# The output projection of a hybrid decoder block, computed as seven block products instead of eight

## The reference

```
x  += (sum_i sigmoid(gate_i) * y_i) @ W_o      # the output projection, 1024 x 1024
x  += squared_relu_mlp(rms_norm(x))            # up: 1024 -> 4096, down: 4096 -> 1024
```

## Time and profile before

| | us |
|---|---|
| median of 3 runs | 1169.45 (1169.36 to 1169.71) |
| time of the profiled execution | 1170.08 |
| its span, first to last instruction | 1168.3 |
| TensorE busy | 1152.2 |
| VectorE / ScalarE / GpSimd busy | 660.6 / 528.6 / 392.4 |

### The profile page before, as it was taken

One profiled execution on the slowest core, in us unless ns is written; L12 is line 12 of the kernel. 1 busy time (PEld: TensorE's weight loads), 2 busy tenths in 40 slices (PEclk: granted clock), 3 DMA queues, 4 the chain that ended last, 5 costly groups with the idle time before them and its releaser, 6 DMA issues.

```text
span 1168.3 us, 20827 instructions
## 1 busy us (share of the span) xinstructions
PE 1152.2 (99%) x8686; PEld 944.8 (81%) x8686; DVE 660.6 (57%) x1202; ACT 528.6 (45%) x848; POOL 392.4 (34%) x256
## 2 busy tenths in 40 slices
PE   8999999999999999999999999999999999999998
PEld 7998877978789678767777777778888888888887
DVE  4699526454554552543253475552469469378386
ACT  6455432323323443677454554442654344344452
POOL 3444426243544225323341543244240420511400
PEclk9999999999999999999999999999999999999999
DMA  6213323122321141211621221243161622534421
GB/s 257 91 57 104 113 83 109 65 82 81 107 73 67 56 140 52 92 36 37 238 76 61 75 91 55 72 163 99 64 234 58 267 90 90 221 104 158 166 91 72
DMA packets 39455, 124.06 MB, mean 106 GB/s; under 512 B 4657, under 2 KB 9521, under 8 KB 38850
## 3 DMA queue, kind: packets, MB, share of 16 engines
q1 hardware_dynamic: 33744, 111.17, 27.8%
q10 hardware_dynamic: 5106, 11.43, 2.8%
q0 software_dynamic: 512, 0.13, 0.1%
HBM read 112.01 MB, written 9.04 MB: 104 GB/s over the span
## 4 chain that ended last, share of the span: by engine, by line
PE 82%; DVE 8%; ACT 5%; POOL 2%; issue 2%; DMA 1%; SPq 0%; DVEq 0%; ACTq 0%; POOLq 0%
PE pst L1993 23%; PE pst L1995 22%; PE pst L1994 22%; POOL w_lo L907 1%; PE pst L2507 1%; ACT w_hi L1026 1%; PE pst L2499 1%; PE pst L2232 1%; PE pst L2285 1%; PE pst L2484 1%; PE pst L2469 1%; DVE cdif L1513 1%; PE pst L2219 1%; DVE x_lo L1847 1%; PE pst L2524 1%
## 5 line engine op out<-in xcount | busy, mean ns | idle before, releaser
L907 POOL TENSOR_TENSOR w_lo<-raw,w_hi 128x1024 fp32r<-128x1024 f32 x109 | 270.5, 2487 | 484.4 <-ACT w_hi L1026 472.7
L1993 PE MATMUL pst<-h_hi,w_hi 128*128 128x512 f32 (+1 forms) x704 | 257.1, 365 | 1.3 <-DVE h_lo L1486 0.7
L1995 PE MATMUL pst<-h_hi,w_lo 128*128 128x512 f32 (+1 forms) x704 | 243.2, 345 | 0.0
L1994 PE MATMUL pst<-h_lo,w_hi 128*128 128x512 f32 (+1 forms) x704 | 242.9, 345 | 0.0
L1993 PEld LDWEIGHTS pst<-h_hi,w_hi 128*128 128x128 f32 x704 | 133.4, 189 | 25.9 <-issue 5.4
L1026 ACT ACTIVATE w_hi<-raw 128x1024 fp32r<-128x1024 f32 x127 | 133.0, 1052 | 44.9 <-PE pst L1995 40.8
L1994 PEld LDWEIGHTS pst<-h_lo,w_hi 128*128 128x128 f32 x704 | 133.6, 190 | 15.7 <-issue 2.9
L1995 PEld LDWEIGHTS pst<-h_hi,w_lo 128*128 128x128 f32 x704 | 133.3, 189 | 16.0
L1993 PE MATMUL pst<-x_hi,w_hi 128*128 128x512 f32 (+1 forms) x272 | 102.6, 377 | 0.4 <-DVE x_lo L1859 0.4
L1994 PE MATMUL pst<-x_lo,w_hi 128*128 128x512 f32 (+1 forms) x272 | 102.4, 377 | 0.0
L1995 PE MATMUL pst<-x_hi,w_lo 128*128 128x512 f32 (+1 forms) x272 | 102.4, 376 | 0.0
(11 more groups left out here) (370 smaller groups left out, 2412.9 us busy)
## 6 DMA issues: line engine op xcount, KB each, us to landing
raw<-in_weights SPq DMA_DIRECT2D x127, 512.0 KB, 3.4
raw_late<-in_weights SPq DMA_DIRECT2D x34, 512.0 KB, 4.2
raw_free<-in_weights SPq DMA_DIRECT2D x27, 512.0 KB, 3.6
xt<-in_x SPq DMA_DIRECT2D x4, 512.0 KB, 6.0
wait_gate<-stage ACTq DMA_DIRECT2D x8, 256.0 KB, 2.6
gate_t<-wait_gate ACTq DMA_DIRECT2D x1, 2048.0 KB, 9.2
x<-in_x ACTq DMA_DIRECT2D x1, 2048.0 KB, 8.5
out<-x SPq DMA_DIRECT2D x7, 256.0 KB, 2.1
```

Source lines behind the costliest of these rows:

```text
L907: nc.gpsimd.tensor_tensor(w_lo[:, u % W_SLOTS, :], raw_unit(u), w_hi[:, u % W_SLOTS, :].bitcast(F32), ALU.subtract).then_inc(lo_ready, 1)
L1993: M(out, lh, rh, start=(first and i == 0), stop=onto, skip_group_check=onto)
L1994: M(out, lh, rl, start=False, stop=onto, skip_group_check=onto)
L1995: last = M(out, ll, rh, start=False, stop=(final and i == len(terms) - 1), skip_group_check=onto)
```

## The change

- The output projection is a sequence of 14 jobs `("wo", -1, (m, j))`, seven products m of two units j, in the form of `down`, with an order of its own: 0 (U11), 1 (S1), 2 (S2), 3 (U12), 4 (S4), 5 (S3), 6 (U22). Each job has 12 matmuls of 512 columns. Below, the units are called F to F+13 (product m has F+2m and F+2m+1). Products 1, 2, 5 and 6 take differences of weight units (F+2 to F+5, F+10 to F+13), made on VectorE by `weight_sums`.
- The low parts of these eight units are written by VectorE, those of the six plain ones (F, F+1, F+6 to F+9) by GpSimd.
- `merge_tile` writes the quarters, and for odd k the four sums and their parts, and then does the weight sums and low parts that are due. For `proj` k that is: the difference of F+2 in `merge_tile(2)`, of F+3 in 4, of F+4 and the low part of F+2 in 6; the first `wo` job brings the difference of F+5 and the low part of F+3.
- Products 0 to 4 complete the first two token blocks, 5 and 6 the others. `norm2` of blocks 0 and 1 stands around product 5, that of 2 and 3 behind product 6, among four units of `up_early` (two before), which have banks of their own.
- The ten raw slots are used from unit F on, and the order of the loads is adapted.

The core of the diff (`merge_tile` is that of VectorE; the waits behind it are TensorE's and, last, those of SP's queue):

```diff
+P1, P5, P6, P2, P7, P3, P4 = ((U11, (0, 0)), (S1, (0, 1)), (S2, (1, 1)), (U12, (1, 0)), (S3, (0, 0)), (S4, (1, 1)),
+                              (U22, (1, 0)))
+PRODUCTS = {"wo": [P1, P5, P6, P2, P3, P7, P4], "down": [P1, P5, P6, P2, P7, P3, P4]}
+LESS = {"wo": {1: 0, 2: 1, 5: 2, 6: 2}, "down": {1: 0, 2: 1, 4: 2, 6: 2}}
+BANKS = {"wo": [(4, 5), (6, 7), (4, 5), (1, 3), (6, 7), (4, 5), (4, 5)],
...
+PHASE_O = [("wo", -1, (m, j)) for m in range(NM) for j in range(2)]
+EARLY = 4
...
+FFN0 = UNIT_NO[("w_o", -1, (0, 0))]
...
+DOWN_NO = {u: i for i, u in enumerate(sorted(UNIT_NO[u] for u in UNITS if u[0] == "w_down" or UNIT_NO[u] in LESS_UNIT))}
...
             g("merge_tile", KD - 1)
-            jobs(KD // 2 + 2)
+            jobs(8)
             g("norm2_tables")
-            for b in range(NB):
...
+            jobs(2)
+            g("norm2", 0)
+            jobs(1)
+            g("norm2", 1)
+            jobs(1)
+            g("norm2_turn", 0)
+            g("norm2_turn", 1)
+            g("norm2_low", 0)
+            jobs(1)
+            g("norm2_low", 1)
+            jobs(1)
+            g("up_units")
+            g("up_early", 0)
+            g("norm2", 2)
+            g("up_early", 1)
+            g("norm2", 3)
+            g("norm2_turn", 2)
+            g("norm2_low", 2)
+            g("up_early", 2)
+            g("norm2_turn", 3)
+            g("norm2_low", 3)
+            g("up_early", 3)
...
             def merge_tile(k):
-                dve.wait_ge(m_hi, k + 1)
-                V.scalar_tensor_tensor(out=x_lo[:, k, :], in0=merged[:, k, :], scalar=0.5,
-                                       in1=x_hi[:, k, :].bitcast(F32), op0=ALU.mult, op1=ALU.subtract)\
-                    .then_inc(m_lo, 1)
+                p, n = k // 2, JOB_NO[("proj", BRANCH_SW, k)]
+                if k % 2 == 0:
+                    dve.wait_ge(u_hi_ready, 3 * p + 1)
+                    V.scalar_tensor_tensor(out=u_lo[:, p, U11, :], in0=merged[:, k, 0:TH], scalar=0.5,
+                                           in1=u_hi[:, p, U11, :].bitcast(F32), op0=ALU.mult, op1=ALU.subtract)\
+                        .then_inc(u_lo_ready, 1)
+                else:
+                    dve.wait_ge(job_out["proj"], 3 * KD + k + 1)
+                    u11, u21, u12, u22 = (merged[:, 2 * p + h // 2, TH * (h % 2):TH * (h % 2) + TH] for h in range(4))
+                    sums = msum[:, p % 2]
+                    link(V.tensor_tensor(sums[:, 0], u21, u22, ALU.add))
+                    link(V.tensor_tensor(sums[:, 1], sums[:, 0], u11, ALU.subtract))
+                    V.tensor_tensor(sums[:, 2], u21, u11, ALU.subtract)
+                    V.tensor_tensor(sums[:, 3], u12, sums[:, 1], ALU.subtract).then_inc(usum_ready, 1)
+                    dve.wait_ge(u_hi_ready, 3 * p + 2)
+                    V.scalar_tensor_tensor(out=u_lo[:, p, U12:U22 + 1, :], in0=halves(merged[:, k, :]), scalar=0.5,
...
+                    dve.wait_ge(u_hi_ready, 3 * p + 3)
+                    V.scalar_tensor_tensor(out=ms_lo[:, p], in0=sums, scalar=0.5, in1=s_hi_[:, p].bitcast(F32),
+                                           op0=ALU.mult, op1=ALU.subtract).then_inc(u_lo_ready, 1)
+                weight_sums(UNIT_NO[units_of(JOBS[n])[0]] + SUM_AHEAD)
+                weight_lows(converted_after(n))
...
-                elif kind == "down":
+                elif kind in ("wo", "down"):
                     m, j = b
...
+                    if j == 0 and onto:
+                        pe.wait_ge(job_out["down"], NM * (a + 1) + ONTO[kind][m] + 1)
+                    if j == 0 and a >= 0 and not onto:
+                        pe.wait_ge(job_out["down"], NM * (a + 1))
                     pe.wait_ge(*low_done(u))
...
...
+                if u == FFN0:
+                    sp.wait_ge(yl_ready, y_count(BRANCH_SW) + 4)
+                if u == FFN0 + RAW_FREE + RAW_SLOTS:
+                    sp.wait_ge(dense_done, JOB_NO[("proj", BRANCH_SW, KD - 1)] + 1)
```

More of the change, by code:

```diff
@@ L151, in source_of @@
 def source_of(u):
-    if u[0] != "w_down":
+    if u[0] not in ("w_o", "w_down"):
         return u
-    (r, q), j = PRODUCTS[u[2][0]][1], u[2][1]
+    (r, q), j = PRODUCTS["wo" if u[0] == "w_o" else "down"][u[2][0]][1], u[2][1]
+    if u[0] == "w_o":
+        return "w_o", r, j, q
     return "w_down", 4 * u[1] + 2 * r + j, q
@@ L208, in pack_weights @@
             m = ps[u[1]][0][:, 256 * u[2]:256 * u[2] + 256]
[L209 to L210 removed]
+        elif u[0] == "w_o":
+            rows = [P * (4 * u[2] + 2 * kk + u[1]) for kk in range(2)]
+            m = np.concatenate([w_o[0][k:k + P, 512 * u[3]:512 * u[3] + 512] for k in rows], 0)
+        elif u[0] == "w_down":
+            m = w_down[0][256 * u[1]:256 * u[1] + 256, 512 * u[2]:512 * u[2] + 512]
         else:
@@ L513, in build @@
         job_out = {k: sem(k + "_out") for k in
-                   ("aq", "ak", "av", "gate", "proj", "wo", "up", "down")}
+                   ("aq", "ak", "av", "gate", "proj", "up", "down")}
         gate_tanh = sem("gate_tanh")
@@ L613, in norm2_psum, with up_bank @@
         def norm2_psum(b, k):
[L615 to L621, removed]
+            return pst[:, [(6, 7), (1, 3), (4, 5), (6, 7)][b][k // 4], P * (k % 4):P * (k % 4) + P]
+        def up_bank(n):
+            _, c, i = JOBS[n]
+            return 2 * job_slot(n) + (1 if c == 0 and 2 <= i < EARLY else 0)
         def raw_unit(u):
@@ L1368, in merge_tile, with up_units @@
                 act.wait_ge(job_out["proj"], 3 * KD + k + 1)
-                A(x_hi[:, k, :], merged[:, k, :], ACT.Copy, scale=0.5).then_inc(m_hi, 1)
+                p = k // 2
+                if k % 2 == 0:
+                    A(u_hi[:, p, U11, :], merged[:, k, 0:TH], ACT.Copy, scale=0.5).then_inc(u_hi_ready, 1)
+                else:
+                    A(u_hi[:, p, U12:U22 + 1, :], halves(merged[:, k, :]), ACT.Copy, scale=0.5).then_inc(u_hi_ready, 1)
+                    act.wait_ge(usum_ready, p + 1)
+                    A(s_hi_[:, p], msum[:, p % 2], ACT.Copy, scale=0.5).then_inc(u_hi_ready, 1)
+            def up_units():
+                high(UP0 + W_SLOTS)
             def norm2(b):
-                if b == 0:
-                    act.wait_ge(m_lo, KD)
-                act.wait_ge(job_out["wo"], NB + b + 1)
+                act.wait_ge(job_out["down"], 5 if b < 2 else NM)
                 link(A(h2n[:, b, :], x2[:, b, :], ACT.Square, accum_out=ss2[:, 0, b:b + 1]))
@@ L1647, in job @@
                         dst = x2_part(rq, t)
-                        last = V.tensor_tensor(dst, pst[:, BANKS[m][t], :], dst, ALU.add)
+                        last = V.tensor_tensor(dst, pst[:, banks[t], :], dst, ALU.add)
                     last.then_inc(job_out["down"], 1)
@@ L2165, in job @@
                             pe.wait_ge(u_lo_ready, operand_split(a, which, p))
-                        last = product3(pst[:, BANKS[m][t], :],
-                                        [(operand(which, p, t), (w_hi[:, us, ws], w_lo[:, us, ws]))],
-                                        p == 0 and m not in ONTO, p == FC // 2 - 1 or m in ONTO, onto=m in ONTO)
+                        last = product3(pst[:, banks[t], :],
+                                        [(operand(kind, which, p, t), (w_hi[:, us, ws], w_lo[:, us, ws]))],
+                                        p == 0 and not onto, p == FC // 2 - 1 or onto, onto=onto)
                         if ends and kk == 1 and t == 0:
```

185 lines of the change are left out of this document (67 added, 118 removed).

## The result

The changed kernel takes 1181.26 us (median of 4 executions, 1180.27 to 1182.50) against 1169.58 for the kernel before (median of 4): ratio 1.0099, interval 1.0087 to 1.0112. It is 1.0% slower, 1.8 us above the forecast of 1179.5 and inside its range.

The account below looks back on a forecast made before the run. VectorE was taken to become the bound from `proj` 3 to product 1; -5.4 + 0.7 - 0.4 + 11.5 + 1.2 + 0.5 + 1.9 = +10.0 us on the median 1169.45 gave 1179.5, range 1170 to 1186.

Parts of the forecast that it names:

- VectorE becomes the bound: Projection stage to product 1: a pair of jobs costs VectorE 7.0 us against TensorE's 5.44; TensorE loses +11.5 us; chance 0.60.
- The two holds: Merge tiles 0 and 2: VectorE waits out low parts running on GpSimd, +2.2 and +1.2 us.
- The low part of F+3: Before product 1's second half: VectorE ends this low part at 809.9, where TensorE unhindered would start at 798.4.
- the wait of `proj` 6: Projection stage: `proj` 6 waits for a bank and starts at 787.7.
- rival B: Same as the main forecast, but TensorE restarts at half the clock after the wait: +13 to +16 us, 1182 to 1185; chance 0.12.
- A: The main forecast: VectorE is the bound from `proj` 3 to product 1, +5 to +14 us; chance 0.60.
- a granted clock below 1.00: Sign of being wrong: the stage's granted clock below 1.00 would point to TensorE restarting at half the clock.
- `up` 4: First `up` jobs: the bank of `up` 2, which `up` 4 needs, is read late; +1.9 us (0 to 3).
- The norm and `h2n`: Behind the projection: second token block ready late, +1.2 us; third block's multiplication perhaps held by GpSimd's low parts, +0.5.
- The matmuls and `up_early`: Output projection loses 24 matmuls, -5.4 us; two more early `up` units run as narrower matmuls, +0.7.
- The dropped wait before the last norm: Last `norm2`: the 0.38 us wait at 836.99 goes, as more split work covers it; -0.4 us.
- Loads: Weight loads in SP's queue: nothing counted; one late load would stop its unit for what it is late.

Follow-up runs that it names:

- experiment 4: The changed kernel with two up units run early instead of four: 1181.68 us, ratio 1.0103.
- experiment 1: The changed kernel without the eight weight-difference subtractions of w_o on VectorE (the output is another): 1174.82 us, ratio 1.0042.
- experiment 2: The changed kernel without the sums of activations, products reading quarters instead (the output is another): 1169.04 us, ratio 0.9993.
- experiment 7: The kernel before, with four unused sums and one unused 128x1024 instruction added on VectorE per odd tile: 1175.17 us, ratio 1.0048.
- experiment 3: The changed kernel with fourteen filler matmuls into an unused bank ahead of the wait before product 1's second half: 1179.51 us, ratio 1.0083.
- experiment 9: The changed kernel with banks of their own for up 4 and up 5: 1183.00 us, ratio 1.0113.
- experiment 8: The changed kernel with the plain U12 product second, the sums written by GpSimd and their low part one tile later on VectorE: 1180.52 us, ratio 1.0094.
- experiment 6: The changed kernel with the plain product of U12 moved from fourth to second place: 1181.05 us, ratio 1.0097.
- experiment 5: The changed kernel with the low parts of the eight w_o difference units on GpSimd too: three executions 1181.60, 1182.05 and 1184.68 us, ratio 1.0113.

## Why the prediction was right, step by step

**VectorE becomes the bound.** Right, in cause and size. It took 3.94 us for an odd tile (forecast 3.96), with the factor 0.5 at no extra cost: 1.23 us for the 128x1024, next start at 1.14. The two holds were 2.2 and 1.1 us (forecast 2.2 and 1.2). The low part of F+3 let TensorE on at 809.22 (forecast 809.9, or 809.45 with this execution's earlier start): 11.3 us late instead of 11.5. The steps before it came within 0.3 us when the 0.45 is allowed for: 783.22 (forecast 783.7), 792.34 (793.0), 800.74 (801.4), 803.01 (803.7). Only the wait of `proj` 6 is missing, since slow matmuls (eight at 0.43 us) had used its time up; in experiment 4, where the clock stayed up there, it is seen: 786.63 us (787.7; that execution came to the stage 0.9 us early), a wait of 0.83. Experiments 1, 2 and 7 show the cause from three sides: a part of the work taken away, another part, and one part added to the kernel before. So does the moment itself: in the changed kernel and experiments 3, 4 and 9 the second half of product 1 starts 42.3 us behind the first `proj` matmul, though the clock fell at other places in each. The two holds are 3.3 us of this path, as forecast; no run took them away, so that share is read from the timeline alone.

**The clock.** The term that the sum did not have. The forecast gave rival B 0.12 as if it excluded A, and named a granted clock below 1.00 as a sign of being wrong. That sign came: B's mechanism stood on top of A, with 3.0 us in the profiled execution (1182.26 us, inside B's range), and by the mean clock of the other three some 1 to 3. Neither reason against it held. That no slice of the trace before shows a fallen clock says nothing, since that trace has no such wait in this stage; and the shorter waits of 2.2 to 2.3 us were followed by it too, in four of six kernels. With it the sum of the profiled execution nearly closes: -5.4 + 0.7 - 0.4 + 11.3 + 3.0 + 0.9 + 1.4 = 11.5 of the 12.2 measured in the stage. Some 0.3 of the rest stands at `up` 4, where the starts (870.26, 871.98, 872.32) make the wait cost 1.7 and not 1.4; the other 0.4 is not attributed. That the forecast came within 1.8 us in spite of the missing term is in part luck: the terms that it had came out 1.5 us too high together (15.1 against 13.6: VectorE 0.2, norm 0.8, `up` 4 0.5). The Trainium skill (TensorE: Matmul & The Clock Gate, Part 1) says that idleness takes the array to 1.2 GHz, and that the same kernel shows different counts of slow matmuls from run to run. The traces agree with the first (0.50 behind the waits above). For the second there are fourteen slow matmuls after a wait of 3.18 us here and six after 3.21 in experiment 4, which are two kernels that are alike up to there; of executions of one kernel only the mean clock speaks (0.996 to 0.999).

**The clock in the projection stage.** It was 0.50 from 785 to 788 us too, behind the wait of 2.26. That is no term of the sum: VectorE was behind, and the wait of `proj` 6 became shorter by what the matmuls took longer.

**The norm and `h2n`.** Forecast +1.2 and +0.5, measured 0.55 and 0.32 of wait. The hold of the multiplication came (3.59 us for two instead of 1.5) and mostly fell in time that TensorE had cover for. The Trainium skill (SBUF — State Buffer, Who interferes with whom) has VectorE and GpSimd exclude each other where VectorE's instruction reads two SBUF operands, or is of a form that takes both ports. The trace agrees with the first: 0.42 became 2.60. The two multiplications read one tile and a column of scalars; their 3.59 fits the second if theirs is such a form, which no run shows.

**`up` 4.** Forecast +1.9, measured 1.44 at the place named. But the bank was not the bound. Experiment 9 took the bank away and a wait of like size appeared behind it at `down` (1.84), where VectorE had been at work since 881.42 with no gap but a few of 0.5 us for ScalarE. So the term looks like that of VectorE's work per `up` pair, felt wherever TensorE first comes up against it; no run took that work away.

**The matmuls and `up_early`.** -5.4 and +0.7 are seen in the spacing, unchanged at 0.227 where the clock is up, and experiment 2, where most waits are gone, returns to the time before with 3.8 us of waits left. The stage from the first `proj` matmul to the last of `w_o` is 9.3 us longer net of transposes (68.2 us before and 78.1 after, with 1.6 and 2.2 of transposes); the forecast had about 6, and the 3.0 of the clock is most of the difference. The dropped wait before the last norm was right in kind: with two early units it comes back as 2.4 us.

**Loads.** No transfer ended a wait of TensorE in the stage, as forecast.

## What to carry to other kernels

A scheme that saves multiplications pays in additions, and they are paid by an engine with a queue of its own. Before taking such a step, lay that engine's work in program order against the point where the first result is wanted; its idle time behind that point can't be used. Here 24 matmuls (5.4 us) were bought with some 19 us of VectorE's work (12.4 for tiles, 6.9 for weights), ahead of a point up to which it had some 9 us free: 6.5 in the projection window and 2.7 from there to 798.4.

Moving work to another engine doesn't relieve the first if its instructions are held by the other's (2.60 for 0.42 us here), or if it waits in order for the result (experiment 8). Experiments 6 and 8 moved the wait and not the time; experiment 5 brought no time either, for a cause that no trace shows. And a wait that has been removed must be looked for again behind its old place before its length is booked as a gain.

Add the clock to the price of any wait of TensorE of some 3 us where it is on the path: another 1 to 3 us here, and it need not be the same from one execution to the next.

## What the runs showed of the hardware

- TensorE's granted clock fell to 0.50 (1.2 GHz) at or behind every single wait of 2.9 us or more that was profiled past the first matmuls (2.91, 3.16, 3.18, 3.21, 3.94, 6.29), in stretches otherwise busy; after the one of 3.16, in experiment 9, only 1.3 us behind its end. At shorter ones it depended on the execution: at the wait of 2.2 to 2.3 us before `proj` 5 it fell at once in experiments 1 and 9, some 1.5 us later in the changed kernel, and not at all in 3, 4 and 6; at the like wait before `proj` 7 it fell at once in 3 and not in 4 and 6. In experiment 9 the clock was at 0.50 from 794 to 797 us, behind a wait of 1.78; behind the 1.84 of experiment 1 it stayed at 1.00. Spacing of 128x512 matmuls went from 0.227 to 0.427 us; where the clock was down at the end of the wait, the first was spaced 0.59.
- How long the matmuls behind the wait stay slow is not set by the length of the wait: 6.4 us after 3.18, 3.0 after 3.21, 3.2 after 3.94, 6.1 after 6.29.
- Fourteen filler matmuls (3.33 us), which use nothing but idle time, kept the clock up behind that wait in the one execution that was profiled.
- GpSimd took 0.72 to 1.6 us for a 128x256 addition that VectorE does in 0.42, and 2.4 for the 128x1024 that VectorE does in 1.2.
